# A decoder layer on one core: products with w_ada in three column groups, a new order of the prologue, and gate projections beside the first tile

## The reference

```
mod = silu(c) @ w_ada + b_ada              # c: 1 + 8 conditioning rows, w_ada: 1024 x 3072
shift, scale, gate = split(mod, 3)
h = rms_norm(x, pre_norm_w) * (1 + scale) + shift
proj = h @ w_in                            # 1024 x 3080: 24 tiles of 128 columns, and 8 gate columns
... pooling mixer on u; causal conv on q,k,v; gated delta rule (chunked) ...
y = concat(y_a, y_b) @ w_out
x = x + gate * rms_norm(y, post_norm_w)
```

## Time and profile before

| what | value |
|---|---|
| median of 3 runs | 1101.53 us (1099.67 to 1102.23) |
| the profiled execution, its own time | 1102.44 us |
| its span in the trace | 1100.6 us |
| TensorE busy | 1066.3 us, 97% |
| VectorE busy | 654.9 us, 59% |
| ScalarE busy | 358.2 us, 33% |
| GpSimd busy | 223.2 us, 20% |
| granted TensorE clock, mean | 0.99 |

### The profile page before, as it was taken

How to read it: one execution, slowest core, us unless ns; L and a number is a source line. 1 busy time by engine, 2 the same in 40 slices (tenths; PEclk the granted TensorE clock), 3 DMA queues, 4 the chain that set the end, 5 groups by cost and what they waited for, 6 DMA issues and landing times.

```text
span 1100.6 us, 16922 instructions
## 1 busy us (share of the span) xinstructions
PE 1066.3 (97%) x6320; PEld 840.8 (76%) x6320; DVE 654.9 (59%) x1382; ACT 358.2 (33%) x713; POOL 223.2 (20%) x226
## 2 busy tenths in 40 slices
PE   7999999989999999999999999999999999999995
PEld 1568757867878888787878888887878888888774
DVE  1669887546436795565356794564255775355654
ACT  3355422233624521132425511143325521112211
POOL 1223344653410011331000012240000010443000
PEclk9989999998999999999999999999999999999998
DMA  9577638434666554323646454224674343222265
GB/s 367 189 271 282 230 135 325 135 116 172 235 253 229 195 188 154 115 79 114 250 163 258 177 188 151 79 93 156 247 260 177 116 153 116 77 79 82 99 236 186
DMA packets 44964, 196.04 MB, mean 178 GB/s; under 512 B 8858, under 2 KB 9626, under 8 KB 27348
## 3 DMA queue, kind: packets, MB, share of 16 engines
q1 hardware_dynamic: 44884, 194.97, 49.4%
HBM read 150.14 MB, written 44.81 MB: 177 GB/s over the span
## 4 chain that ended last, share of the span: by engine, by line
PE 63%; DVE 2%; POOL 2%; issue 2%; DVEq 0%; ACT 0%; POOLq 0%; ACTq 0%
PE acc L2002 12%; PE acc L2004 11%; PE acc L2003 11%; PE ring L2044 7%; PE ring L2031 2%; PE ring L2032 2%; PE ring L2033 2%; PE acc L2031 2%; PE acc L2033 2%; PE acc L2032 2%; PE ring L2198 2%; PE ring L2061 1%; PE ring L2070 1%; PE ring L2071 1%; POOL win L1828 1%
## 5 line engine op out<-in xcount | busy, mean ns | idle before, releaser
L2002 PE MATMUL acc<-hhi,wsl 128*128 128x512 f32 x768 | 316.4, 412 | 1.1 <-DVE y L1295 1.1
L2004 PE MATMUL acc<-hhi,wsl 128*128 128x512 f32 x768 | 301.2, 392 | 0.0
L2003 PE MATMUL acc<-hlo,wsl 128*128 128x512 f32 x768 | 300.6, 391 | 0.0
L2002 PEld LDWEIGHTS acc<-hhi,wsl 128*128 128x128 f32 x768 | 145.3, 189 | 33.8 <-issue 5.1
L2004 PEld LDWEIGHTS acc<-hhi,wsl 128*128 128x128 f32 x768 | 144.8, 188 | 32.0
L2003 PEld LDWEIGHTS acc<-hlo,wsl 128*128 128x128 f32 x768 | 145.4, 189 | 27.1 <-issue 1.4
L1181 DVE SCALAR_TENSOR_TENSOR cacc<-raw,cw,cacc 128x512 f32<-128x512 f32 x144 | 114.8, 797 | 5.1
L1788 POOL TENSOR_TENSOR wsl<-wraw,wsl 128x512 fp32r<-128x512 f32 x64 | 87.0, 1377 | 139.4 <-ACT wsl L865 139.4
L894 ACT ACTIVATE raw<-acc 128x512 f32<-128x512 f32 x48 | 28.6, 597 | 164.6 <-PE acc L2004 164.5
L1089 DVE TENSOR_TENSOR hlo<-htmp,hhi 128x512 fp32r<-128x512 f32 x32 | 22.2, 692 | 62.2 <-ACT hhi L839 61.9
L1178 DVE TENSOR_SCALAR cacc<-raw,cw 128x512 f32<-128x512 f32 x48 | 23.5, 490 | 56.3 <-ACT raw L894 53.9
(11 more groups left out here) (305 smaller groups left out, 1793.6 us busy)
## 6 DMA issues: line engine op xcount, KB each, us to landing
wsl<-kept_w SPq DMA_DIRECT2D x96, 1024.0 KB, 4.8
kept_w<-wsl SPq DMA_DIRECT2D x32, 1024.0 KB, 6.5
wraw<-in_w SPq DMA_DIRECT2D x64, 256.0 KB, 3.8
wada<-in_w_ada SPq DMA_DIRECT2D x8, 1024.0 KB, 13.0
xb<-in_x SPq DMA_DIRECT2D x16, 512.0 KB, 5.9
xres<-in_x SPq DMA_DIRECT2D x16, 512.0 KB, 5.8
out_y<-ytok SPq DMA_DIRECT2D x16, 512.0 KB, 8.0
wada<-in_w_ada SPq DMA_DIRECT2D x16, 256.0 KB, 4.8
```

The source lines that it names most:

```text
L2002: nc.tensor.matmul(acc[t % 2][:], w[:, 0, k], hi[:, k], start=(k == 0), stop=False)
L2003: nc.tensor.matmul(acc[t % 2][:], w[:, 0, k], lo[:, k], start=False, stop=False)
L2004: last = nc.tensor.matmul(acc[t % 2][:], w[:, 1, k], hi[:, k], start=False, stop=(k == KT - 1))
```

## The change

- **Three column groups.** `cpad` holds the 9 conditioning columns padded to 32. k step k of a w_ada product goes to partitions 32g to 32g+31 of the bank, g = k mod 3, so that three partial sums stand in 96 partitions. `row_copy` copies 96 partitions, and the turn becomes a product with `fold` (96 x 9, three unit matrices), which also adds the three. The same holds for the gate pieces: ScalarE now copies the two `ada` banks to `cacc` in slot 1, and VectorE adds three partial rows in slots 3 and 4 (four operations for each row instead of two); the spreading moves to slots 5 and 6.
- **Order of loads.** `xb` right behind `cin`, then piece 0, small tables (five of them moved up), piece 1, three weight halves, the sampled rows, pieces 2 and 3.
- **Scaling of `xb`** by two engines: row tiles 0 and 1 on VectorE, 2 and 3 on ScalarE. An `Exp` on a small table moves up behind it.
- **First tiles by k step:** tiles 0 and 1 alternate for k steps 0 to 3, with the products of pieces 2 and 3 and the transposes among them.
- **Gate projections** in block 0 two k steps' worth at a time behind each of the k steps 4 to 7 of tile 0; VectorE's copy of them comes before the convolution of tile 0. What VectorE does with the sampled rows (`sample_rows`) moves from the prologue to behind the convolution of tile 2.

```
+GR = 3
-GATE_ROW = {1: 0, 2: 1}
-GROW_AT = {4: 0, 5: 1}
+GATE_COPY = 1
+GATE_ROW = {3: 0, 4: 1}
+GROW_AT = {5: 0, 6: 1}
...
+            for i in range(4):
+                sp.dma_start(xb[:, i], a["x"][0][:, i]).then_inc(x_in.sem, 16)
             modulation(0)
-            modulation(1)
...
+            act.wait_ge(*rx_f(PROLOGUE, 0))
+            for t in range(2, 4):
+                nc.scalar.activation(xb[:, t], xb[:, t], ACT.Copy, scale=rx[:, t:t + 1]).then_inc(xn.sem, 1)
...
+            halves_hi(0)
+            halves_hi(1, range(1))
+            act.wait_ge(sm_x0, 16)
+            act.wait_ge(*xsq(PROLOGUE, 3))
+            nc.scalar.activation(junk[0:NS, :], xrow, ACT.Square, accum_out=s8[:, 0:1]).then_inc(*step("act", "x_sq"))
...
+                    if it == 0 and slot == GATE_COPY:
+                        for m in range(2):
+                            act.wait_ge(s_gate, m + 1)
+                            nc.scalar.activation(cacc[0:GR * BS, m], bank("ada", m)[0:GR * BS, :], ACT.Copy).then_inc(s_ada, 1)
...
+                nc.vector.tensor_copy(rows96[j], mod_bank[j][0:GR * BS, :]).then_inc(s_rows, 1)
+
+            front_xn(dve, PROLOGUE, range(2))
             row_copy(0)
...
-                nc.vector.tensor_tensor(grow[:, cols], grow[:, cols], bank("ada", m)[0:1 + NS, :], ALU.add).then_inc(s_trc, 1)
-                dve.wait_ge(s_trc, 2 * m + 1)
+                for g in range(GR):
+                    if g:
+                        dve.wait_ge(s_trc, (GR + 1) * m + g)
+                    nc.vector.tensor_tensor(grow[:, cols], grow[:, cols], cacc[g * BS:g * BS + 1 + NS, m], ALU.add
+                                            ).then_inc(s_trc, 1)
+                dve.wait_ge(s_trc, (GR + 1) * m + GR)
...
+                    if t == GATES and it == 0:
+                        gate_sums(it)
                     convolve(it, t)
...
-                    last = nc.tensor.matmul(acc[j % 2][0:1 + NS, :], cin[:, k, :], wada[j][:, k], start=(k == 0),
-                                            stop=(k == KT - 1))
+                    g = k % GR
+                    last = nc.tensor.matmul(mod_bank[j][g * BS:(g + 1) * BS, :], cpad[:, k], wada[j][:, k], start=(k < GR),
+                                            stop=(k >= KT - GR))
...
+                for k in range(2):
+                    for t in range(2):
+                        tile(0, t, k)
+                modulate(2, 1)
+                modulate(3, 0)
                 for t in range(2):
-                    for k in range(4):
-                        tile(0, t, k)
+                    tile(0, t, 2)
+                modulate(3, 1)
+                for m in range(4, 7):
+                    front_pe(pe, PROLOGUE, m)
+                for t in range(2):
+                    tile(0, t, 3)
+                turn_rows(2)
+                turn_rows(3)
                 front_pe(pe, PROLOGUE, 7)
-                for t in range(2):
-                    for k in range(4, KT):
-                        tile(0, t, k)
+                pe.wait_ge(s_pre, 3)
+                bank_free(pe, 0, "gates")
+                for k in range(4, KT):
+                    tile(0, 0, k)
+                    gates(0, (k - 4, k))
+                for k in range(4, KT):
+                    tile(0, 1, k)
```

More of the change, by code:

```diff
@@ L407, in layer_kernel @@
         pwr = gpw[0:1 + NS]
-        rows9 = [t[0:1 + NS, j] for t in (tmpa, pooled) for j in range(2)]
+        rows96 = [t[0:GR * BS, j] for t in (tmpa, pooled) for j in range(2)]
+        fold = sb("fold", [GR * BS, 1 + NS])
         ssx = sb("ssx", [P, 4]); rx0 = sb("rx0", [P, 4]); rx = sb("rx", [P, 4])
@@ L1486, in sample_out, with sample_rows, gate_sums @@
                 nc.vector.tensor_tensor(ssm[:, m], ssm[:, m], heads(bank("sop", m)), ALU.add).then_inc(*s(f"sn{m}"))
+            def sample_rows():
+                dve.wait_ge(*done("pe", "hs"))
+                nc.vector.tensor_tensor(hs[:], row_bank[:, 0:64].rearrange("p (k s) -> p k s", k=KT), amul[:, :, 1:1 + NS],
+                                        ALU.mult).then_inc(*step("dve", "h0"))
+                dve.wait_ge(*done("dve", "h0"))
+                nc.vector.tensor_tensor(hs[:], hs[:], mod[:, 0:8, 1:1 + NS], ALU.add).then_inc(*step("dve", "h"))
+                dve.wait_ge(*done("dve", "h"))
+                nc.vector.tensor_copy(hs2[:, :, 0:NS], hs[:]).then_inc(*step("dve", "hh"))
+                dve.wait_ge(*done("dve", "hh"))
+                nc.vector.tensor_tensor(hs2[:, :, NS:], hs[:], hs2[:, :, 0:NS].bitcast(F32), ALU.subtract).then_inc(*step("dve", "hl"))
+                dve.wait_ge(s_const, 64)
+                nc.vector.tensor_copy(gpick[:], gsel[:, 0:NC]).then_inc(s_pre, 1)
+            def gate_sums(it):
+                dve.wait_ge(*job["gates"](it, 0))
+                dve.wait_ge(*job["gb"](it, -1))
+                nc.vector.tensor_copy(gsb[:], bank("gates")[0:16, :]).then_inc(g_c.sem, 1)
             def gated(it, t):
@@ L1520, in block_of @@
                         blocks(it)
+                    if t == GATES and it == 0:
+                        gate_sums(it)
                     convolve(it, t)
-                    if t == GATES:
-                        dve.wait_ge(*job["gates"](it, 0))
-                        dve.wait_ge(*job["gb"](it, -1))
-                        nc.vector.tensor_copy(gsb[:], bank("gates")[0:16, :]).then_inc(g_c.sem, 1)
+                    if t == GATES and it:
+                        gate_sums(it)
+                    if t == GATES + 2 and it == 0:
+                        sample_rows()
                     if t == GATES + 1:
@@ L1962, in gate_rows_of @@
                 for k in range(KT):
-                    last = nc.tensor.matmul(bank("ada", j)[0:1 + NS, :], cin[:, k, :], wada[4 + j][:, k], start=(k == 0),
-                                            stop=(k == KT - 1))
+                    g = k % GR
+                    last = nc.tensor.matmul(bank("ada", j)[g * BS:(g + 1) * BS, :], cpad[:, k], wada[4 + j][:, k],
+                                            start=(k < GR), stop=(k >= KT - GR))
                 last.then_inc(s_gate, 1)
@@ L2006, in tile, with gates @@
                     last.then_inc(proj.sem, 1)
+            def gates(it, ks):
+                for k in ks:
+                    nc.tensor.matmul(bank("gates")[0:16, :], wg2[:, k], hhi[:, k], start=(k == 0), stop=False)
+                    mm = nc.tensor.matmul(bank("gates")[0:16, :], wg2[:, k], hlo[:, k], start=False, stop=(k == KT - 1))
+                if k == KT - 1:
+                    mm.then_inc(job["gates"].sem, 1)
             def out_tile(it, m):
@@ L2169, in block_of @@
                         pe.wait_ge(s_pre, 4)
-                    if t == GATES:
+                    if t == GATES and it:
                         bank_free(pe, it, "gates")
-                        for k in range(KT):
-                            nc.tensor.matmul(bank("gates")[0:16, :], wg2[:, k], hhi[:, k], start=(k == 0), stop=False)
-                            mm = nc.tensor.matmul(bank("gates")[0:16, :], wg2[:, k], hlo[:, k], start=False,
-                                                  stop=(k == KT - 1))
-                        mm.then_inc(job["gates"].sem, 1)
+                        gates(it, range(KT))
                     if t == GATES + 1:
@@ L2325, in layouts @@
         "gsel": pick,
+        "fold": np.tile(np.concatenate([np.eye(1 + NS), np.zeros((BS - 1 - NS, 1 + NS))]), (GR, 1)).astype(np.float32),
         "c_all": np.concatenate([f("c_prompt"), f("c_sample")]).T.reshape(KT, P, 1 + NS).transpose(1, 0, 2),
```

144 lines of the change are left out of this document (67 added, 77 removed).

## The result

| | median | runs | lowest to highest |
|---|---|---|---|
| before | 1100.67 us | 5 | 1099.67 to 1102.23 |
| changed | 1095.11 us | 5 | 1092.88 to 1096.51 |

The ratio is 0.9945, with a 95% interval of 0.9934 to 0.9957: 5.6 us faster. The forecast was 1091.5, about 10 us faster; the time lies in its range of 1086.5 to 1099.5, but only half of the gain came. The profiled execution took 1095.11 us (span 1093.3).

What follows compares the result with a forecast made beforehand. TensorE, busy 97% of the span, was taken as the bound. 8.3 us by tile 3 + 3.3 at the gate pieces - 0.7 clock - 1.0 slots = 9.9 us off 1102.44; median forecast 1091.5 us, range 1086.5 to 1099.5.

Steps and rivals of the forecast that it cites:

- Cost of a product in three groups: w_ada products on TensorE: three groups overlap fully, half a piece 1.7 us instead of 3.4, gate pieces 5.2 instead of 13.8.
- Rival A: w_ada products: the groups don't run together, tile 2 starts near 64 as before; about 1099 us, chance 0.11.
- Input chain: Prologue: xb lands at 9.2, scaling starts at 15.5 and ends at 18.2, transposes and turn end at 20.2 us.
- This is the place where the new order itself waits (2 us): Prologue: weights' low parts come late, so tile 1's first k step comes at 29.8 us, tile 0's possible at 27.5.
- TensorE's row to tile 2: Prologue: TensorE full from 29.8 to 42.6, waits for hlo until 44.9, tile 2 at 55.8 instead of 63.99 us.
- What the clock takes back: Prologue gaps on TensorE may bring half clock: 2.5 us taken, between 0 and 5, leaving 8.3 us at tile 3.
- 10.8 us earlier at best: Start of tile 3 with the prologue's gain, the stop at gt gone and full clock, before the clock's deduction.
- Gate pieces: Before tiles 12 to 16: TensorE saves 8.6 us, VectorE lets 3.3 count; 0.7 taken off for the clock.
- Slots 3 and 4: VectorE's eight gate_row operations, 2.7 us in each slot: 1 us of delay taken, between 0 and 2.7.
- The sum: Whole kernel: 8.3 + 3.3 - 0.7 - 1.0 = 9.9 us faster, 14.1 without deductions; 1091.5 us.
- Rival B: More given back: both gaps and tile 15's wait lower the clock, slots 3 and 4 cost 2.7; 1097.5 us, chance 0.14.
- Rivals C and D: C: clock stays half until tile 2, up to 1112 us, 0.06; D: VectorE already the bound, about 1101, 0.06.

Runs made afterwards that it cites:

- undo_all_groups: Changed kernel without any column groups, pieces 0 to 3 and the gate pieces in one group each; 1107.67 us, ratio to before 1.0070.
- after_again: The changed kernel itself run and profiled a second time, nothing altered; 1095.91 us, ratio to before 0.9958.
- x_after_0: Changed kernel with the input loaded behind piece 0 instead of ahead of it; 1098.76 us, ratio to before 0.9990.
- scale_dve: Changed kernel with all four row tiles of xb scaled by VectorE, none by ScalarE; 1095.12 us, ratio to before 0.9956.
- lo_first: Changed kernel with GpSimd's low parts of the first three weight halves ahead of the sampled rows' root; 1092.54 us, ratio to before 0.9935.
- lo_turn: lo_first plus, on TensorE, the turn of piece 2 right behind k step 2 and piece 3's behind k step 3; 1089.72 us, ratio 0.9904.
- undo_gate_groups: Changed kernel with only the two gate pieces back in one column group; 1098.59 us, ratio to before 0.9988.

## Why the prediction was right, and where it was not

**Direction, bound and range: right.** TensorE was busy for 96% of the span and its row set the end, but for tiles 12 to 16, where VectorE was the later engine, as forecast.

**Cost of a product in three groups: right, and a little better.** 32 records in 5.34 us, against 13.90: 2.60 times less, where 5.2 us had been taken. A record costs 0.167 us in place of 0.434. The Trainium skill (TensorE: Matmul & The Clock Gate, Measured speedup vs the span model) gives 2.38; the measurement is above it and decides here. Rival A is out. Its price was wrong too: 1099 was said, undo_all_groups took 1107.67. It had forgotten that piece 0 then ends only at 20.97 and that half of piece 2 stands ahead of the first tile, which came at 36.53 and not at 31.

**Input chain: right within 1 us.** Squares from 9.60 (9.2 said), scaling at 15.87 (15.5), transposes at 18.16, `mod` from 25.65. `htmp` had been put at 25.4; in after_again, where `amul` wasn't held, it started at 26.36. That the input should come first was worth 3.5 to 5 us (x_after_0). Two scaling engines were worth nothing (scale_dve), and the 5.49 / 4 us a row tile rested on a row that held a port wait.

**"This is the place where the new order itself waits (2 us)": the step that failed.** The forecast had seen that GpSimd's low parts come late, behind the root of the sampled rows, and took it as a delay of tile 1's weights alone. What they delayed was VectorE: 3.84 us on `amul`, or 3.0 us on the cast in the other execution. `htmp` started at 30.06 in the first; the first tile at 32.18 in place of 27.5. lo_first takes it away and starts the tile at 29.02.

**TensorE's row to tile 2: sizes off.** A turn with `fold` is eight records and about 1 us (0.95 to 1.06), two of them 1.85, where a turn had been 0.41 in the earlier trace rows and was priced so. Then came the wait for `hhi` of group 4, forecast as 2.3 us and measured as 1.99. Had the turns stood apart, as in lo_turn, it would have been 0.62.

**What the clock takes back: half of the mechanism, and the size was inside its bounds.** 2.5 us were taken, with 0 and 5 as ends, for half clock behind the 2.3 us gap. That came, behind the second wait. The other fall, at 27.3 us, stands behind a wait of 1.09 us, and the forecast had taken one of 0.95 us as free. In the profiled execution those sixteen matmuls started 0.43 us apart in place of 0.23, some 3 us together; in the other execution the windows from 30 to 60 us read 0.98, 0.89 and 0.96, about a third of that. At tile 3 the forecast had 8.3 us; the two executions gave 3.84 and 6.39. The port hold, the second wait and the two stretches at half clock make the gap; lo_turn, which has little of any of them, has tile 3 at 62.33, 10.5 us earlier than before, close to the "10.8 us earlier at best".

**Gate pieces: exact.** 3.3 us of the 8.6 were to be kept, and 7.11 - 3.84 = 3.27 were; undo_gate_groups gives 3.2. TensorE's waits for `zmul` were 1.12 and 3.17 us (5.3 and a longest of 3.5 had been said). The 0.7 us for the clock there did not come in time, though the clock did fall: behind the wait of 3.17 us the six matmuls of tile 15 at half clock took some 1.2 us more. VectorE was the later engine, and tile 16 followed the third `zmul` as soon as it could. In after_again the same wait (3.14 us) was followed by full clock, and TensorE waited another 1.33 us for that `zmul` instead.

**Slots 3 and 4: 1 us was said, nothing can be seen.** The eight operations took 9.0 us with GpSimd beside them (three in 3.10) and not 5.4, but TensorE waited only 0.6 us between 173 and 200. From the third `zmul` to the end are 928.5 us before, 928.3 and 929.6 in the changed kernel's two executions, and 928.1 and 929.0 in the two kernels that have half of these operations. Whatever it costs is below what executions differ by.

**The sum.** By the profiles: 3.84 + 3.27 and 0.2 for the end are the 7.3 us by which the spans differ; 1.8 of them are how far the profiled execution of before lay above its median, which leaves about the 5.6 of the medians. Rival B (the gain given back, 1097.5) came nearest in time, but not by its own reasons: it asked for 2.5 us by the clock at tile 15 and 2.7 us in slots 3 and 4. The clock did fall at tile 15, but under VectorE's work, and the 2.7 us aren't there. Rivals C and D did not happen: the half clock that began at 27.3 us ended at 34.1 and did not last to tile 2, and tile 16 followed tile 3.

## What to carry to other kernels

Before an instruction is moved on GpSimd's queue, look at which short SBUF-to-SBUF instruction of VectorE will stand beside it: a step of 0.2 us on the critical path was held for 4, and moving a root of eight numbers behind the low parts took nearly all of the hold away (0.52 us were left). Products with few stationary columns (9 of 128 here), which leave most columns of the array empty, can be run in three column groups at 2.6 times the rate, and most of their saving counts where they stand in the bound engine's row (9.5 to 11 of nearly 15 us for pieces 0 to 3); elsewhere only the wait of the engine that takes over counts (3.3 of 8.6 us). Keep independent work for the stretch behind the last serial turn: starting the tiles earlier gained nothing while the wait and the clock behind it stayed.

## What the runs showed of the hardware

- VectorE was held until the last of three consecutive instructions of GpSimd was over, not only the one under way: 4.04 us for `amul` (0.20 alone), 3.43 us for a cast (0.42). In before it was two of them, and 3.49 us for a 128x1024 scaling (0.75).
- No length of a wait tells by itself what the clock does. A wait of 1.98 or 1.99 us in the prologue was followed by half clock in all nine traces that have it. Of the waits ahead of tile 15, 3.17 us in the changed kernel's first execution was followed by half clock, and 3.14 us in its second by a granted clock of 1.00; so it was in lo_first and scale_dve (3.14 and 3.13 us). In lo_first and lo_turn, whose instructions are the same up to 30 us, the half piece behind a wait of about 1 us took 1.90 us in the one and 3.57 in the other, with a clock of 1.00 and 0.83 from 20 to 30 us. What decides it stays open, and the stretch at half clock differs between executions.
- A turn by a 96 x 9 product costs 0.12 us a record, eight records, where the four transposes before took 0.41 us in all.
